# A four-block float32 model on one core: four weight units carried through norms 7 and 9, GpSimd's sums in them, and transposes ahead of three stretches

## What is computed

```python
def rmsnorm(x, w):
    y = xf * lax.rsqrt(jnp.mean(xf * xf, axis=-1, keepdims=True) + RMS_EPS)
    return y * w
...
h = rmsnorm(x, ffn_pre_norm)                    
up = causal_dwconv(h @ w_ffn_up, ffn_conv_w, ffn_conv_b)
f = (gelu(f_gate) * f_val) @ w_ffn_down
...
h = rmsnorm(x, gain)
(q, k, v, decay_rank, g, ...) = split(h @ w_in_even)
log_a = log_sigmoid(decay_rank @ gla_w_up + gla_b_up) / 16
```

## Time and profile before

| What | Value |
|---|---|
| median of 3 runs (lowest to highest) | 1828.88 us (1827.12 to 1832.87) |
| the profiled execution: its time, its span | 1827.75 us, 1825.7 us |
| mean granted PE clock, of 2.4 GHz | 0.901 |
| busy: PE, PE weight load, DVE, ACT, POOL | 80%, 54%, 39%, 32%, 2% |
| chain that ended last, by engine | DMA 44%, PE 36%, DVE 15%, ACT 2%, issue 1% |

### The profile page before, as it was taken

The page is one execution under the profiler, slowest core; times in us unless marked ns, Lnnn a source line. Parts: engine busy times, 40 slices in busy tenths (PEclk is TensorE's granted clock), DMA queues, the critical chain, the costliest instruction groups (busy, mean ns, idle before and its releaser), DMA issues.

```text
span 1825.7 us, 25122 instructions
## 1 busy us (share of the span) xinstructions
PE 1455.1 (80%) x10456; PEld 985.8 (54%) x10456; DVE 707.2 (39%) x1257; ACT 588.5 (32%) x1011; POOL 35.6 (2%) x40
## 2 busy tenths in 40 slices
PE   6999995556656566656656567999999999999998
PEld 4788831111111111112111113998998999999997
DVE  4566600000000000000000000997996998478764
ACT  6444410000000000000000001677476776565654
POOL 0000200000000000000000000000000000000201
PEclk9999897888787886787887877999999999999999
DMA  9566799999999999999999999657453755555330
GB/s 399 221 249 248 308 396 428 429 429 429 428 430 427 429 429 428 430 427 429 429 428 429 428 429 428 235 184 208 159 182 137 273 204 187 185 174 173 139 139 24
DMA packets 53266, 573.55 MB, mean 314 GB/s; under 512 B 4928, under 2 KB 15424, under 8 KB 16576
## 3 DMA queue, kind: packets, MB, share of 16 engines
q1 hardware_dynamic: 47440, 563.10, 76.0%
q10 hardware_dynamic: 5744, 9.28, 1.5%
HBM read 568.04 MB, written 4.33 MB: 314 GB/s over the span
## 4 chain that ended last, share of the span: by engine, by line
DMA 44%; PE 36%; DVE 15%; ACT 2%; issue 1%; SPq 0%; DVEq 0%; ACTq 0%
PE bank L1645 36%; DMA ring<-in_w_gate 14%; DMA ring<-in_w_up 14%; DMA ring<-in_w_down 14%; DVE ring_rounded L2443 6%; DVE work L930 2%; DVE work L748 1%; DMA ring<-in_dense 1%; DVE work L920 1%; DVE work_rounded L2366 1%; DMA work<-decay_rows 1%; ACT work L2126 1%; DVE work L739 1%; ACT weights_high_rounded L2126 1%; DVE work L938 1%
## 5 line engine op out<-in xcount | busy, mean ns | idle before, releaser
L1645 PE MATMUL bank<-ring,work 128*32 128x512 f32 x3008 | 486.3, 781 | 296.4 <-DMA ring<-in_w_up 123.1
L1645 PEld LDWEIGHTS bank<-ring,work 128*32 128x32 f32 x3008 | 94.1, 127 | 652.5 <-DMA ring<-in_w_up 205.8
L2126 ACT ACTIVATE work<-bank 128x512 f32<-128x512 f32 (+3 forms) x156 | 73.9, 489 | 998.9 <-PE bank L1645 666.7
L2443 DVE TENSOR_TENSOR ring_rounded<-ring,weights_high_rounded 128x1024 fp32r<-128x1024 f32 x208 | 252.7, 1220 | 79.7 <-ACT weights_high_rounded L2126 79.7
L2126 ACT ACTIVATE weights_high_rounded<-ring 128x1024 fp32r<-128x1024 f32 x244 | 254.0, 1051 | 42.7 <-PE bank L1645 41.4
L2711 DVE TENSOR_TENSOR work<-work,bank 128x512 f32<-128x512 f32 x16 | 16.5, 1030 | 588.4 <-PE bank L1645 588.4
L1645 PE MATMUL bank<-h_high_rounded,weights_high_rounded 128*128 128x256 f32 x1264 | 184.9, 285 | 3.2 <-ACT h_high_rounded L2126 1.8
L1645 PE MATMUL bank<-h_high_rounded,ring_rounded 128*128 128x256 f32 x1264 | 174.4, 277 | 0.6 <-DVE ring_rounded L2454 0.6
L1645 PE MATMUL bank<-h_normed_rounded,weights_high_rounded 128*128 128x256 f32 x1264 | 173.7, 278 | 0.0
L1645 PEld LDWEIGHTS bank<-h_high_rounded,weights_high_rounded 128*128 128x128 f32 x1264 | 161.2, 188 | 13.7 <-issue 7.2
L1645 PEld LDWEIGHTS bank<-h_high_rounded,ring_rounded 128*128 128x128 f32 x1264 | 158.3, 188 | 1.0 <-DVE ring_rounded L2454 0.8
(11 more groups left out here) (267 smaller groups left out, 1193.1 us busy)
## 6 DMA issues: line engine op xcount, KB each, us to landing
ring<-in_w_gate SPq DMA_DIRECT2D x63, 2048.0 KB, 16.1
ring<-in_w_down SPq DMA_DIRECT2D x63, 2048.0 KB, 16.1
ring<-in_w_up SPq DMA_DIRECT2D x61, 2048.0 KB, 16.4
ring<-in_dense SPq DMA_DIRECT2D x60, 2048.0 KB, 8.3
ring<-in_w_ada SPq DMA_DIRECT2D x12, 2048.0 KB, 13.4
work<-in_w_up SPq DMA_DIRECT2D x3, 1024.0 KB, 14.5
bias_diagonals<-work SPq DMA_DIRECT2D x2, 1536.0 KB, 15.1
ring<-in_dense SPq DMA_DIRECT2D x2, 1024.0 KB, 18.7
```

The source lines that it names most:

```text
L1645: return nc.tensor.matmul(o, lhsT, rhs, start=start, stop=stop)
L2126: return nc.scalar.activation(o, i, f, **kw)
L2443: v.tensor_tensor(as_r(w), w, w_high[:, buffer, :], ALU.subtract).then_inc(s.w_low, 1)
```

## The change

Head 7 and head 9 take four units instead of two (`dense_through_norm`, `TOGETHER = 4`), and their norms move to GpSimd's sums, in bank 6. Of the four units, two have their low weights inside the loop over the tiles, the other two between the token sums and the spread of the roots. Unit 4 of each goes to a bank of its own (4 or 5), so that it waits for nobody's reading. DVE copies the spread row from PSUM into RS (`KEPT_ROWS`), and the low weights of up unit 4 move ahead of the first tap. In the even layer the product of the decay rank comes behind unit 4, and the two transposes of RS and ACT's copy of them go. Two transposes of the identity are put at the end of both heads, ahead of even unit 5, of the odd layer and of odd unit 12, and one float32 matmul of ones ahead of head 7.

```diff
-ADDED_NORMS = {2: KT - 2, 4: 2, 6: KT - 2, 8: KT - 2, 10: KT - 2, 11: KT - 2}
+ADDED_NORMS = {2: KT - 2, 4: 2, 6: KT - 2, 7: KT - 2, 8: KT - 2, 9: KT - 2, 10: KT - 2, 11: KT - 2}
-TOKEN_NORMS = {2: 7, 4: 4, 6: 6, 8: 6, 11: 6}
+TOKEN_NORMS = {2: 7, 4: 4, 6: 6, 7: 6, 8: 6, 9: 6, 11: 6}
+KEPT_ROWS = (7, 9)
+TOGETHER = 4
...
+            def dense_through_norm(units, early, high, low, base, norm, spare):
...
+                for k in range(KT + 1):
+                    if k < KT:
+                        pe.wait_ge(s.act_high, base + k + 1)
+                        for _, _, bank, counts in units:
+                            if k == 0:
+                                pe.wait_ge(s.w_high, counts)
+                            mm(bank[:, 0:SEQ], w_high[:, (counts - 1) % HIGHS, k * P:(k + 1) * P], high[k], k == 0, False)
+                        if k < KT - 1:
+                            for unit in units[:early]:
+                                low_weights(unit, (k,))
+                    if k:
+                        pe.wait_ge(s.act_low, base + k)
+                        for _, _, bank, counts in units:
+                            mm(bank[:, 0:SEQ], w_high[:, (counts - 1) % HIGHS, (k - 1) * P:k * P], low[k - 1], False, False)
+                for unit in units[:early]:
+                    ends(unit, low_weights(unit, (KT - 1,)))
+                added_token_sums(norm)
+                for unit in units[early:]:
+                    ends(unit, low_weights(unit, range(KT)))
+                spread_roots(norm, spare, 0, 0)
+                for _ in range(2):
+                    nc.tensor.transpose(spare[:, SEQ:SEQ + P], ident, ident)
...
-            dense_together([(d2_block(u), u % UNITS, B[(PU2 + u) % 4], D1_UNITS + u + 1) for u in range(L_UP, L_UP + 2)], *normed, IN_AT["up"][0], norm=7)
-            for u in range(2, 2 * FT):
-                unit2(L_UP + u, normed)
+            mm(B[7][:, SEQ:SEQ + P], ones[:], ones[:])
+            dense_through_norm([(d2_block(u), u % UNITS, B[(PU2 + u) % 4], D1_UNITS + u + 1) for u in range(L_UP, L_UP + TOGETHER)], 2, *normed, IN_AT["up"][0], norm=7, spare=B[5])
+            pe.wait_ge(s.toep_sb, 3)
+            for u in range(TOGETHER, 2 * FT):
+                tensor_dense2(pe, dense_unit, L_UP + u, normed, PU2 + L_UP + u, bank=B[4] if u == TOGETHER else None)
...
             root(7)
+            for u in range(2):
+                unit_done(d2_block(L_UP + u), block_ends(L_UP + u))
+                weight_high(D1_UNITS + L_UP + u + AHEAD2)
...
                 scaled(u)
                 if u:
+                    if u == 1:
+                        weight_low(L_UP + AHEAD2)
                     tap(u - 1, 1)
-                    weight_low(L_UP + u - 1 + AHEAD2)
+                    if u > 1:
+                        weight_low(L_UP + u - 1 + AHEAD2)
                     tap(u - 1, 2)
...
-            even(2, 3)
-
-            pe.wait_ge(s.norm_inverted, 10)
-            for t in range(TT):
-                last = nc.tensor.transpose(B[5][:, t * P:(t + 1) * P], RS[:, 1, t * P:(t + 1) * P], ident)
-            last.then_inc(s.gl_mm, 1)
+            tensor_dense2(pe, dense_unit, L_EVEN + TOGETHER, normed, pu3(L_EVEN + TOGETHER), bank=B[5])
+
             pe.wait_ge(s.dense_sb, pu3(L_EVEN) + 1)
...
-            even(4, 5, 6, 7, 8, 9, 10)
+
+            def transposes_before(unit):
+
+                pe.wait_ge(s.dense_sb, pu3(unit) - 3)
+                for _ in range(2):
+                    nc.tensor.transpose(B[pu3(unit) % 4][:, 0:P], ident, ident)
+
+            transposes_before(L_EVEN + 5)
+            even(5, 6, 7, 8, 9, 10)
...
             added_sums(10)
+            transposes_before(L_ODD)
...
             logits(*causal, range(4, AH))
+            transposes_before(L_ODD + 12)
             odd(*range(12, 17))
...
-            act.wait_ge(s.gl_mm, 1)
-            link(fn(TOKEN_RSTD, B[5][:, 0:SEQ].rearrange("p (t c) -> p t c", t=TT)[:, :, 0], ACT.Copy))
...
-            copy_values3(0, L_EVEN + 11, 4, AV, TOKEN_RSTD)
+            copy_values3(0, L_EVEN + 11, 4, AV, TOKEN_ROOTS)
...
-            add_squares(6)
-
-            add_squares(8)
-            add_squares(10)
+            for i in (6, 7, 8, 9, 10):
+                add_squares(i)
...
                     dve.wait_ge(s.norm_spread, list(TOKEN_NORMS).index(i) + 1)
+                    if i in KEPT_ROWS:
+                        link(v.tensor_copy(RS[:, i % 2, :], rstd_row(i)))
```

More of the change, by code:

```diff
@@ L460, in tensor_block2 @@
             dense_together([(d2_block(u), u % UNITS, B[(PU2 + u) % 4], D1_UNITS + u + 1) for u in range(2)],
-                           *normed, IN_AT["in2"][0], norm=5, low_weights_last=True)
+                           *normed, IN_AT["in2"][0], norm=5)
             def in2(*units):
@@ L1018, in values3 @@
                         s.ring_used if t == TT - 1 else s.dense_mm, 1)
-            dense_together([(d2_block(u), u % UNITS, B[pu3(u) % 4], D1_UNITS + u + 1) for u in range(L_EVEN, L_EVEN + 2)],
-                           *normed, IN_AT["even"][0], norm=9)
+            dense_through_norm([(d2_block(u), u % UNITS, B[pu3(u) % 4], D1_UNITS + u + 1) for u in range(L_EVEN, L_EVEN + TOGETHER)],
+                               2, *normed, IN_AT["even"][0], norm=9, spare=B[5])
             def logits(kind, q_of, k_of, heads):
@@ L1187, in copy_values3 @@
                     else:
[L1188 removed]
+                        fn(dst[:, t, :], src, ACT.Copy, scale=scale[:, 2 * t:2 * t + 1]).then_inc(s.dense_sb, 1)
             raw_splits(3 * KT, HH_plain, EVEN_GAIN)
@@ L1675, in dense_unit, with dense_together @@
                 return ins
-            def dense_together(units, high, low, base, norm, low_weights_last=False):
+            def dense_together(units, high, low, base, norm):
                 def low_weights(k):
@@ L1698, in dense_together @@
                             at = slice((k - 1) * P, k * P)
-                            done = k == KT and not low_weights_last
-                            last = mm(bank[:, 0:SEQ], w_high[:, (counts - 1) % HIGHS, at], low[k - 1], False, done)
-                            if done:
-                                last.then_inc(s.ring_used if sub == UNITS - 1 else s.dense_mm, 1)
+                            mm(bank[:, 0:SEQ], w_high[:, (counts - 1) % HIGHS, at], low[k - 1], False, False)
                         column_sum(norm, k - 1)
-                for block_no, sub, bank, counts in units if low_weights_last else ():
+                for block_no, sub, bank, counts in units:
                     pe.wait_ge(s.w_low, counts)
```

47 lines of the change are left out of this document (28 added, 19 removed).

## The result

| What | Before | After |
|---|---|---|
| median of 7 runs | 1827.65 us | 1834.94 us |
| ratio, 95% interval | | 1.0039, 1.0027 to 1.0051 |
| profiled execution: span, mean granted PE clock | 1825.7 us, 0.901 | 1833.1 us, 0.901 |

The change makes the kernel 0.39% slower, 7 us. The forecast was 1829.8 with 1833.5 as its upper end; of the cases that it priced only the least likely one, 1835.0, reached so far.

The account below looks back on a forecast made before the run. DVE was taken to bound the stretch behind head 7, PE that behind head 9. Terms +1.0 +1.1 -0.9 -0.2 gave +1.0 us, a median of 1829.8 against 1828.88; own range 1828 to 1832, full range 1826.0 to 1833.5.

Parts of the forecast that it names:

- all of DVE's delay reaches 1542.49: Behind head 7: DVE bounds the chain to the junction (down projection's last tile of first product), so its +1.0 us counts fully.
- ends in waits: Behind head 7: PE's earlier start at unit 4 is lost waiting for low weights and at the junction.
- Head 7: From the loop to the junction: net +0.6 us, with GpSimd's 0.4 +1.0 us.
- The steps from the loop to the first scaled unit: Head 7: sums, 16 low-weight matmuls, spread and copy put the first scaled unit at 1413.55, not 1412.08: +1.47 us.
- GpSimd's hold: In the head's loop: six adds hold DVE 0.3 us each; token sums come 0.4 us later, bounds 0 and 3.0.
- DVE's holes: Start of head 7's up units: two DVE waits, 0.40 and 0.47 us, close through the moved weights: -0.87 us.
- Behind the last scaled unit: After the up stretch, to norm 8's sums: nothing added beyond head 7's delay.
- Rival (b): Two transposes don't set PE's pace; 1.1 and 0.35 come back, +2.5 us, 1831.4; chance 0.12.
- Rival (c): PE's longer waits at the junction and ahead of unit 7's low weights lower the clock: +3.6 us, 1832.5; chance 0.1.
- Rival (d): GpSimd holds DVE for each whole add: sums 3.0 us later, +2.6 a head, +6.2 in all, 1835.0; chance 0.06.
- Head 9: Even layer: later gate product delays unit 7's low weights by 1.4 us, less 0.35 from pace: +1.1 us.
- Odd layer: Transposes turn PE to the faster pace: units 0 to 9 -0.9 us, units 12 to 16 -0.2 us.

Follow-up runs that it names:

- e2: Changed kernel with one GpSimd add in place of six in norms 7 and 9 (five tiles' squares missing from those sums); 1833.70 us, ratio 1.0026.
- f2: Changed kernel with two more transposes ahead of the down projection's second tile; 1832.75 us, ratio 1.0028.
- i2: Head 7 as in h1 plus the change's moved weights for units 4 and 5, head 9 as in g4, odd layer's transposes; 1827.19 us, ratio 0.9988.
- h4: Changed kernel with the late tile's three products taken last in the third unit of the down projection's first tile; 1832.94 us, ratio 1.0022.
- e1: Changed kernel without the two transposes ahead of up unit 4; 1833.61 us, ratio 1.0030.
- e4: Changed kernel with two float32 products of ones in place of the two transposes ahead of up unit 4; 1836.23 us, ratio 1.0033.
- g2: Changed kernel with the gate product (decay rank) ahead of even unit 4; 1833.77 us, ratio 1.0030.
- g3: Changed kernel with the spread of the roots behind the first eight of the sixteen low-weight products, in both heads; 1833.16 us, ratio 1.0025.
- g4: Changed kernel with the edits of g1, g2 and g3 together; 1832.20 us, ratio 1.0011.
- e3: Kernel before with only the odd layer's two pairs of transposes, ahead of its units 0 and 12; 1828.62 us, ratio 0.9996.
- f3: Kernel before with only two transposes ahead of up unit 2; 1827.89 us, ratio 0.9996.
- f4: Changed kernel with head 7 as it was before, head 9 and all later transposes as in the change; 1830.71 us, ratio 1.0006.
- h1: Kernel before with the late tile's three products taken last in the third unit of the down projection's first tile; 1826.77 us, ratio 0.9988.
- f1: e1 with twelve float32 products of ones ahead of the last tile of the down projection's first product; 1835.37 us, ratio 1.0038.
- h2: g4 with the late tile taken last as in h1; 1826.76 us, ratio 0.9992.
- g1: Changed kernel with DVE's low weights of up unit 4 made in its wait for the spread of norm 7; 1834.45 us, ratio 1.0036.

## Why the prediction was wrong

**The step that failed** is the sentence that all of DVE's delay reaches 1542.49 and that what PE wins "ends in waits", with PE's pace in the up stretch taken for given. Head 7 was forecast at +1.0 up to the junction and nothing behind it; up to sums 8 it measured 207.34 - 201.56 = +5.8 in the profiled execution, and the first scaled unit came 3.0 us later, not 1.3 to 2.0. By its own terms:

- The steps from the loop to the first scaled unit, forecast +1.47 without GpSimd: **+1.5** (e2 13.46, before 11.95; one add is still in it, and it made PE wait 0.2 us in the loop). Right, with that much of luck in it.
- GpSimd's hold, forecast 0.4, bounds 0 and 3.0: **1.2** (14.68 in f2 against 13.46). That the adds hold DVE was right; the size per add and the path to PE were not. I took 0.3 us from the nearest row; six adds delayed DVE's last low part by 9.65 - 7.18 = 2.5 us, 0.41 each. I set against it a slack of 1.4 at the last low part. That 2.5 - 1.4 is 1.1 is luck: in f2 that part was there 0.4 us before PE came to it. PE had lost its time earlier, twice in the middle of the loop (0.41 us here, 0.44 at 1405.95), waiting for a high part that ACT could make only behind a held addition of DVE (rows of f2):

```profile
1401.57 0.77 DVE L2476 TENSOR_TENSOR x_resid<-x_resid,work 128x256 f32<-128x256 f32 x1
...
1402.38 0.51 ACT L2175 ACTIVATE h_high_rounded<-x_resid,params 128x256 fp32r<-128x256 f32 x1 [1.13 <-DVE x_resid L2476]
...
1402.94 0.74 PE L1663 MATMUL bank<-h_high_rounded,weights_high_rounded 128*128 128x256 f32 x4 [0.41 <-ACT h_high_rounded L2175]
```

  The rule of the Trainium skill (SBUF — State Buffer, "Who interferes with whom"), that the one that comes first keeps the port for its whole instruction, agrees in kind with the 1.00 us of a low part that takes 0.49 alone. In size the hold in f2 was 0.5 us of the add's 0.74 at a low part and 0.35 at an addition.
- The clock at its lower level in the loop: +0.3, not of the change.
- DVE's holes, forecast -0.87: nothing in the profile after, 0.9 in i2. At the slow pace PE is the bound: DVE's first to last scaled unit took 139.69 - 14.95 = 124.7 us, as before (136.73 - 11.95 = 124.8), though its own waits had become shorter; at the fast pace of h4 it took 138.77 - 14.62 = 124.2.
- Behind the last scaled unit, forecast 0: **+2.8** (67.65 us against 64.83). 24 units at 117.8 in place of 113.3 ns, 576 x 4.5 = 2.6 us, and the junction that no longer waits or helps.

These five make +5.8. **Rival (b)** had the pace as an open cause, but priced it only where the change adds transposes (+1.1 and 0.35), not where a whole stretch of 1600 matmuls had it already. That was the largest exposure in the case: 1600 x 4.5 ns is 7 us, of which 2.8 came through, and the range had none of it.

**Rival (c)** is the other face of this. In the five profiles where the new head ran fast and PE had nothing to fill its wait (e1, e4, g2, g3, g4), it stood 3.1 to 3.3 us, as the prediction had put it ("over 3"), and the clock fell at each. From the end of that wait to sums 8 it was 60.7 us (g3, e4) or 60.8 (g4) against 59.2 before, 1.5 lost where 1.3 was forecast; with 6.8 us at the lower level (e1) 61.9, 2.7 lost. It didn't fall at waits of 1.2 to 1.7 us at this place (before, e3, f3, f4, h4), and h4 against e4, one profile each, shows what filling the wait is worth. The length of a single wait is not the whole of it: ahead of the row with 0.63 the kernel before had two shorter ones close together:

```profile
1371.00 0.69 PE L1645 MATMUL bank<-work_rounded,weights_high_rounded 128*128 128x256 f32 x2 [1.16 <-ACT work_rounded L2126]
1373.15 0.39 PE L1645 MATMUL bank<-work_rounded,weights_high_rounded 128*128 128x256 f32 x1 [1.46 <-ACT work_rounded L2126]
```

The Trainium skill (TensorE: Matmul & The Clock Gate, "Why this matters for your kernels") warns of long idle gaps between bursts; the waits of over 3 us agree. So the changed kernel pays either way: at the slow pace 2.8 us in the down stretch, at the fast one the wait and the clock. I gave this 0.1, and as an alternative to the pace, not as what the pace turns into.

**Rival (d)** came nearest in time, 1835.0, for a reason that is a third of the truth: the adds cost 1.2 us in head 7 and 1.0 in head 9 (e2's even stretch, 116.09, against f2's 117.12).

**Head 9**, forecast +1.1: **+2.1** (116.77 - 114.67). The gate product came 17.69 us behind the loop's start (1629.62 - 1611.93) against 15.23; in e2 16.74. So the order on PE is 1.5, forecast 1.3, and the adds are 1.0, forecast 0.2 to 0.3: the same term mis-sized again, by the same path (PE waits 0.43 and 0.45 us inside this loop too). That the chain through DVE decides was right: unit 7's wait of 1.58 us stood where it was forecast, and g2, which moves the product alone, had the whole loss back. The fast pace of three units, forecast from the transposes ahead of unit 5, did not hold from there: two groups of unit 5 were fast, the rest of it and unit 6 slow, and the last three units fast again, behind unit 7's wait (-0.3). Of the fourteen other profiles with the new head 9 six had their last three units fast.

**Odd layer**, forecast -0.9 and -0.2: **-0.9** from norm 10's sums to the transposes of the earlier trace rows (54.67 us against 55.59), of which 0.3 is lost again behind them in a longer wait of PE, -0.6 to the end. The sign was right, the size half right. The first pair gave 0.8. The second won 0.16 up to those transposes and lost more than that behind them, as the bounds of the prediction had allowed. That the pair sets the pace is not borne out: in e3, with the same transposes, units 0 to 11 stayed slow.

## To carry to other kernels

Where a trace shows a steady stretch at one of two paces, price the whole stretch at the other before you touch what stands ahead of it; the exposure is its length, not the size of the edit. Work that is won on an engine ahead of a wait makes the wait longer, and a longer wait of PE can cost the clock as well: give the waiting unit the products that are ready, and take the late tile last (h1, h4). A sum moved to GpSimd into a loop in which DVE has no gap costs DVE the overlap, here 0.4 us an add.

## What was not expected of the hardware

Rounded 128x256 matmuls with weight loads run from start to start at 113.3 or at 117.8 ns at the same granted clock of 1.00, and stay there for hundreds: 1616 in a row in the changed kernel. The instructions don't decide it. Up to the junction the changed kernel, f2, g2 and h4 issue the same instructions; two ran the up stretch slow, two fast. So do e1 and f1, one fast, one slow. The old head ran it fast in all eight profiles, the new one slow in six of twelve. In the odd layer the groups right behind the pair of transposes ahead of unit 0 were fast in 16 of 17 profiles and behind the pair ahead of unit 12 in 17 of 17, at the same places without it in none of three; in three of the 16 (g2, g4, h2) the pace turned slow again some units later. So transposes go with the fast pace in the odd layer, with e3 as the exception, and neither bring it nor hold it elsewhere: f2 turned slow behind a pair, and g2, g4 and h2 ran slow right behind the pair ahead of even unit 5. What tips PE from one to the other is **open**: f2 turned in a group of low weights, g1 was slow from the first group on with no wait ahead of it. How often the changed kernel's unprofiled runs were slow can't be said.
